# Stick-breaking prompt attention: one sigmoid and value differences in place of two sigmoids and a product

## What is computed

```
z = einsum('bqhd,bshd->bhqs', q, k) * 64 ** -0.5          # valid where s < t
log_keep = where(valid, log_sigmoid(-z), 0)
log_rest = cumsum(log_keep, reverse) - log_keep
a = where(valid, exp(log_sigmoid(z) + log_rest), 0)
o = einsum('bhqs,bshd->bqhd', a, v)
```

## Time and profile before

| | |
|---|---|
| median of three runs | 1863.23 us |
| profiled execution, its own time | 1862.8 us |
| its span, first to last instruction | 1861.1 us |
| granted TensorE clock, mean | 0.969 |
| PE / PEld busy share of the span | 92% / 87% |
| DVE / ACT / POOL busy share | 42% / 26% / 33% |

### The profile page before, as it was taken

How to read it: one execution, slowest core, us unless ns; L and a number is a source line. 1 busy time by engine, 2 the same in 40 slices (tenths; PEclk the granted TensorE clock), 3 DMA queues, 4 the chain that set the end, 5 groups by cost and what they waited for, 6 DMA issues and landing times.

```text
span 1861.1 us, 33169 instructions
## 1 busy us (share of the span) xinstructions
PE 1715.9 (92%) x14512; PEld 1612.1 (87%) x14512; DVE 772.6 (42%) x956; ACT 492.9 (26%) x938; POOL 610.9 (33%) x340
## 2 busy tenths in 40 slices
PE   4999999997988758878999999999999999999998
PEld 3998989995556447767999999999999999999898
DVE  5553033556888457883134222222222121226322
ACT  5232113225766535532132000000000000003211
POOL 4232322322332022324234444444443343442520
PEclk9999999998999968997999999999999999999999
DMA  5112311114000444533321111111111111112221
GB/s 174 49 47 70 101 62 61 66 58 140 1 2 1 149 93 103 114 71 74 91 59 45 46 46 46 46 46 46 46 46 46 46 46 46 46 46 69 57 57 49
DMA packets 202662, 116.50 MB, mean 63 GB/s; under 512 B 74449, under 2 KB 196765, under 8 KB 202525
## 3 DMA queue, kind: packets, MB, share of 16 engines
q1 hardware_dynamic: 193024, 101.45, 19.3%
q10 hardware_dynamic: 9500, 13.02, 1.9%
HBM read 92.60 MB, written 21.84 MB: 61 GB/s over the span
## 4 chain that ended last, share of the span: by engine, by line
PE 77%; DVE 8%; issue 5%; ACT 4%; SPq 3%; DMA 3%; POOL 1%; ACTq 0%; DVEq 0%; POOLq 0%
PE psum L2127 44%; PE psum L1938 8%; PE psum L2419 5%; PE psum L1907 3%; PE psum L1908 3%; PE psum L1909 3%; PE psum L1969 2%; PE psum L1977 2%; PE psum L1990 2%; DVE area L1668 2%; DMA area<-x_scratch 1%; PE psum L2438 1%; DVE area L1509 1%; DVE act_lo L1810 1%; DVE area L1672 1%
## 5 line engine op out<-in xcount | busy, mean ns | idle before, releaser
L2127 PE MATMUL psum<-act_hi,w_round 128*128 128x352 f32 x1920 | 368.5, 325 | 0.7 <-ACT area L1329 0.4
L954 POOL TENSOR_TENSOR w_round<-w_plain,ones 128x1024 fp32r<-128x1024 f32 x80 | 169.8, 2122 | 512.2 <-DMA w_plain<-in_w_up_dram 227.1
L2127 PEld LDWEIGHTS psum<-act_hi,w_round 128*128 128x128 f32 x1920 | 320.6, 189 | 1.8 <-issue 1.0
L2127 PE MATMUL psum<-hid_hi,w_round 128*128 128x352 f32 x1344 | 257.6, 323 | 0.4 <-DVE hid_lo L1840 0.4
L2127 PEld LDWEIGHTS psum<-hid_hi,w_round 128*128 128x128 f32 x1344 | 222.4, 188 | 0.7 <-DVE hid_lo L1840 0.7
L1817 DVE TENSOR_TENSOR area<-psum,area 128x1056 f32<-128x1056 f32 x72 | 90.6, 1258 | 309.5 <-PE psum L2127 309.5
L2127 PE MATMUL psum<-act_lo,w_round 128*128 128x352 f32 x960 | 207.0, 324 | 0.0
L955 POOL TENSOR_TENSOR w_round<-w_plain,w_round 128x1024 fp32r<-128x1024 f32 x80 | 204.3, 2554 | 6.3
L1428 ACT ACTIVATE hid_hi<-area 128x1056 fp32r<-128x1056 f32 x28 | 30.5, 1088 | 589.1 <-DVE area L1833 589.1
L1907 PE MATMUL psum<-w_round,act_hi 128*128 128x256 f32 (+1 forms) x576 | 166.1, 288 | 6.7 <-POOLq L904 3.6
L1908 PE MATMUL psum<-w_round,act_hi 128*128 128x256 f32 (+1 forms) x576 | 163.4, 284 | 0.0
(11 more groups left out here) (298 smaller groups left out, 2666.3 us busy)
## 6 DMA issues: line engine op xcount, KB each, us to landing
w_plain<-in_w_up_dram SPq DMA_DIRECT2D x32, 512.0 KB, 3.9
w_plain<-in_w_down_dram SPq DMA_DIRECT2D x32, 512.0 KB, 3.4
w_plain<-in_w_in_dram SPq DMA_DIRECT2D x14, 1024.0 KB, 5.4
conv_scratch<-area ACTq DMA_DIRECT2D x12, 512.0 KB, 2.7
area<-in_x_prompt_dram SPq DMA_DIRECT2D x8, 512.0 KB, 3.6
w_plain<-in_cache_k_dram SPq DMA_DIRECT2D x4, 1024.0 KB, 5.4
w_plain<-in_w_out_dram SPq DMA_DIRECT2D x8, 512.0 KB, 5.0
w_plain<-in_x_prompt_dram SPq DMA_DIRECT2D x8, 512.0 KB, 4.7
```

What stands on the lines that cost most here:

```text
L954: own.link(pool.tensor_tensor(hi, ring_raw(n), ones[:, 0:1].to_broadcast([P, RB]), ALU.mult))
L2127: last = pe.matmul(bank(bank_set(tile) + c)[:, 0:CH], w(k), a(k)[:, CH * c:CH * (c + 1)], start=(begins and k == ks[0] and w is w_h and a ...
```

## The change

It removes the query stage, the second sigmoid and the product. `keep_buf` after the running product holds R itself, is transposed, and multiplies the differences of neighbouring values, v_(s-1) - v_s (`v_diff`, with zero before the first); one product of v with the identity adds the query's own value. `v_diff` is loaded by SP from the stored `v_out`, shifted by a row, in two transfers (127 rows of the first block, then seven blocks), and POOL subtracts `v_tok` from it in eight instructions of 128x512. The scores of both heads of a pair are computed by one call from the two 64-row halves of `q_t` and `k_t`, the loop over u inside that over 512 columns. Buffers move: `keep_buf` is four deep; two `turned_buf` lie elsewhere; so the first loads of the convolution's values, and two memsets on POOL, move behind the attention, and the scratch clears wait for the differences.

```
-        DEEP = 3
-        sig_buf = carve(act_hi_plain, 0, DEEP, TP)
+        DEEP = 4
+        v_diff = carve(act_hi_plain, 0, NT, W)
...
             sp.wait_ge(dense_ready, NC)
+            sp.wait_ge(v_stored, 32)
+            sp.dma_start(v_diff[1:P, 0, :], v_out[0:P - 1, :]).then_inc(vs_loaded[0], 16)
+            sp.dma_start(v_diff[:, 1:NT, :], v_out[P - 1:TP - 1, :].rearrange("(t p) c -> p t c", p=P))\
+              .then_inc(vs_loaded[1], 16)
             cache_values_in(0)
...
             sp.wait_ge(cs_stored, 1 + 32 * NC)
-            conv_v_in(0)
-            conv_v_in(1)
...
             conv_qk_in(0)
             sums_in(0)
+            conv_v_in(0)
+            conv_v_in(1)
...
-            for y in range(STEPS):
-                pool.wait_ge(scores_ready, 1 + earlier(y, 2))
-                pool.tensor_tensor(q_stage[rows, u, :], q_t[rows, i, P * t:P * (t + 1)], ones[rows, :],
-                                   ALU.mult).then_inc(q_staged, 1)
+            for n in range(NT):
+                pool.wait_ge(vs_loaded[n > 0], 16)
+                pool.tensor_tensor(v_diff[:, n, :], v_diff[:, n, :], v_tok[:, n, :], ALU.subtract).then_inc(d_made, 1)
...
                 act.activation(keep_buf[:, n, 0:w], z, ACT.Sigmoid, scale=-(HD ** -0.5))
-                act.activation(sig_buf[:, n, 0:w], z, ACT.Sigmoid, scale=HD ** -0.5).then_inc(sig_made, 1)
...
             for y in range(STEPS):
+                copy_weights(y)
                 if y + DEEP < STEPS:
                     sigmoids(y + DEEP)
-                if y + 1 < STEPS:
-                    copy_weights(y + 1)
...
-                own.link(dve.tensor_tensor_scan(back, back, starts, 0.0, ALU.mult, ALU.max))
-                dve.tensor_tensor(sig[:, 0:w - 1], sig[:, 0:w - 1], keep[:, 1:w], ALU.mult).then_inc(att_made, 1)
+                dve.tensor_tensor_scan(back, back, starts, 0.0, ALU.mult, ALU.max).then_inc(att_made, 1)
...
+            def scores(t):
+                i, w = t // NT, P * (t % NT + 1)
                 for c in range(0, w, 512):
                     n = min(512, w - c)
+                    for u in range(2):
+                        last = pe.matmul(bank(2 * u + c // 512)[:, 0:n],
+                                         q_t[half(u), i, P * (t % NT):P * (t % NT + 1)],
+                                         k_t[half(u), i, c:c + n], start=True, stop=True)
...
             def values(t):
+                pe.wait_ge(o_split, 1 + max(t - 1, 0))
+                for u in range(2):
+                    pe.matmul(bank(6 + t % 2)[half(u), 0:P], v_tok[:, t % NT, first:first + HD], ident[:],
+                              start=True, stop=False)
                 pe.wait_ge(att_placed, 1 + 2 * t + 2)
+                if i == 0:
+                    pe.wait_ge(d_made, t + 1)
...
+            for t in range(STEPS // 2):
+                turn_weights(2 * t)
+                if t + 2 < STEPS // 2:
+                    scores(t + 2)
+                turn_weights(2 * t + 1)
+                if t:
+                    values(t - 1)
```

More of the change, by code:

```diff
@@ L215, in trunk_step @@
         tails_stored = sem("tails_stored")
-        q_staged = sem("q_staged")
+        vs_loaded = [sem("vs_loaded0"), sem("vs_loaded1")]
+        d_made = sem("d_made")
         scores_ready = sem("scores_ready")
@@ L361, in trunk_step @@
         assert SW == 2 * (TP + TS // 2) and 4 * TS == P
-        DEEP = 3
-        sig_buf = carve(act_hi_plain, 0, DEEP, TP)
+        DEEP = 4
         keep_buf = carve(act_lo_plain, 0, DEEP, TP)
[L367 to L370, removed]
+        v_diff = carve(act_hi_plain, 0, NT, W)
+        turned_buf = [w_plain[:, at:at + TP] for at in (2 * BLK, 2 * BLK + TP, 3 * BLK, 4 * BLK + 528)]
         PARTS = 5
@@ L406, in trunk_step @@
         d_lane_t = carve(dn_w, 5632, LB * LB)[0:LANES, :]
-        g_rows = carve(dn_w, 5632, P)[0:NTT * H, :]
+        g_rows = carve(dn_w, 6016, P)[0:NTT * H, :]
         own_key = carve(dn_w, 3072, TP)
@@ L852, in _ @@
             own = Chain(pool, pool_own)
-            pool.sem_inc(q_staged, 1)
             pool.memset(param_rows, 0.0).then_inc(consts_made, 1)
@@ L918, in _ @@
                 own.leave(2)
-            own.link(pool.memset(q_stage, 0.0))
-            for y in range(STEPS):
-                i, u, t = y // UNITS, y % 2, y % UNITS // 2
-                pool.wait_ge(scores_ready, 1 + earlier(y, 2))
-                pool.wait_ge(q_staged, 1 + y)
-                rows = slice(HD * u, HD * (u + 1))
-                pool.tensor_tensor(q_stage[rows, u, :], q_t[rows, i, P * t:P * (t + 1)], ones[rows, :],
-                                   ALU.mult).then_inc(q_staged, 1)
[L929 to L941, removed]
+            pool.wait_ge(dense_ready, NC)
+            own.mark(pool.memset(own_key[:, 0:TP - P], 0.0))
+            own.mark(pool.memset(v_diff[0:1, 0, :], 0.0))
+            own.link(pool.tensor_copy(own_key[:, TP - P:TP], ident[:]))
+            pool.sem_inc(consts_made, 1)
+            for n in range(NT):
+                pool.wait_ge(vs_loaded[n > 0], 16)
+                pool.tensor_tensor(v_diff[:, n, :], v_diff[:, n, :], v_tok[:, n, :], ALU.subtract).then_inc(d_made, 1)
+            pool.memset(zeros, 0.0).then_inc(consts_made, 1)
+            pool.wait_ge(consts_made, 5)
+            pool.wait_ge(o_ready, 1 + STEPS // 2)
+            own.mark(pool.memset(d_cqk[:, :, TS:HD], 0.0))
+            own.link(pool.memset(d_cv[:, 0, :, TS:HD], 0.0))
             def split_ring(n):
@@ L1146, in sigmoids @@
                 n, w = y % DEEP, P * (y % UNITS // 2 + 1)
-                act.wait_ge(scores_ready, 1 + y + 1)
-                act.wait_ge(att_turned, 1 + earlier(y, DEEP))
+                act.wait_ge(scores_ready, 1 + y // 2 + 1)
+                if y >= DEEP:
+                    act.wait_ge(att_turned, 1 + y - DEEP + 1)
                 z = psum[:, 2 * (y % 2):2 * (y % 2) + 2, :].rearrange("p b c -> p (b c)")[:, 0:w]
-                act.activation(keep_buf[:, n, 0:w], z, ACT.Sigmoid, scale=-(HD ** -0.5))
-                act.activation(sig_buf[:, n, 0:w], z, ACT.Sigmoid, scale=HD ** -0.5).then_inc(sig_made, 1)
+                act.activation(keep_buf[:, n, 0:w], z, ACT.Sigmoid, scale=-(HD ** -0.5)).then_inc(sig_made, 1)
             def round_out(t):
@@ L1182, in _ @@
                 act.wait_ge(k_stored[u], 16 * NTT)
-            copy_weights(0)
             for y in range(STEPS):
+                copy_weights(y)
                 if y + DEEP < STEPS:
                     sigmoids(y + DEEP)
-                if y + 1 < STEPS:
-                    copy_weights(y + 1)
-                if y and y % 2 == 0:
+                if y >= 2 and y % 2:
                     round_out(y // 2 - 1)
@@ L1564, in _ @@
                 n, w = y % DEEP, P * (y % UNITS // 2 + 1)
-                keep, sig = keep_buf[:, n, :], sig_buf[:, n, :]
+                keep = keep_buf[:, n, :]
                 dve.wait_ge(sig_made, 1 + y + 1)
@@ L1962, in _ @@
                     last.then_inc(dense_ready, 1)
[L1963 to L1966, removed]
+            def scores(t):
+                i, w = t // NT, P * (t % NT + 1)
+                if t:
+                    pe.wait_ge(sig_made, 1 + 2 * t)
                 for c in range(0, w, 512):
                     n = min(512, w - c)
-                    last = pe.matmul(bank(2 * u + c // 512)[:, 0:n], q_stage[:, u, :], k_t[:, i, c:c + n],
-                                     start=True, stop=True)
+                    for u in range(2):
+                        last = pe.matmul(bank(2 * u + c // 512)[:, 0:n],
+                                         q_t[half(u), i, P * (t % NT):P * (t % NT + 1)],
+                                         k_t[half(u), i, c:c + n], start=True, stop=True)
                 last.then_inc(scores_ready, 1)
@@ L1977, in turn_weights @@
                     last = pe.transpose(bank(4 + n // 4)[:, P * (n % 4):P * (n % 4 + 1)],
-                                        sig_buf[:, y % DEEP, P * n:P * (n + 1)], ident[:])
+                                        keep_buf[:, y % DEEP, P * n:P * (n + 1)], ident[:])
                 last.then_inc(att_turned, 1)
@@ L1983, in values @@
                 i = t // NT
+                pe.wait_ge(o_split, 1 + max(t - 1, 0))
+                for u in range(2):
+                    first = P * i + HD * u
+                    pe.matmul(bank(6 + t % 2)[half(u), 0:P], v_tok[:, t % NT, first:first + HD], ident[:],
+                              start=True, stop=False)
                 pe.wait_ge(att_placed, 1 + 2 * t + 2)
-                pe.wait_ge(o_split, 1 + max(t - 1, 0))
+                if i == 0:
+                    pe.wait_ge(d_made, t + 1)
                 for n in range(t % NT + 1):
-                    rows = P - 1 if n == t % NT else P
                     for u in range(2):
                         first = P * i + HD * u
```

(21 more changed lines are left out.)

## The result

The change makes the kernel faster: 1845.23 us (median of four runs, 1842.63 to 1845.92) against 1863.31; the ratio is 0.9905, 95% interval 0.9888 to 0.9922, so 18 us or 0.95%. The forecast was 1837, 26 us less, in a range from 1820 to 1856. The profiled execution took 1842.63 us, its span 1840.9, which is 20.2 under the span of before.

What follows compares the result with a forecast made beforehand. PE was taken to set the attention's pace, with DVE close behind, and to be the sole bound afterwards. Three later pairs gain 22.5 us and the first 3.5: 26 off 1862.8 gives 1837, own range 1830 to 1849, stated range 1820 to 1856.

Steps and rivals of the forecast that it cites:

- The halves run side by side: Attention scores: two heads' products in 64-row halves run together, two for the price of one, 9.2 us less per pair.
- The list: PE prices by number n of 128-key blocks: scores .21 + .21n us, transposes .19 + .11n, value products .15 + .22n.
- the charge for the change of shape: PE, per query block: one idle of .17 us charged to the scores for changing into row halves.
- The price of a later pair: Attention's later head pairs: PE 32.4 us plus 1.6 of copy wait, 34.0, 7.5 less than 41.5; three pairs 22.5.
- The check of the list: PE prices summed over a pair of the kernel before, n = 1 to 8: 37.1 us against 37.3 measured.
- rival 1: Attention pairs: better overlap, less PE idle, cheaper shape changes; pair near 30.5 us, 39 us saved, about 1824; chance .13.
- DVE and ACT have room: Later pair: DVE falls to 22.3 us, ACT to some 19; PE alone bounds, the others have 10 us of room.
- The first pair: First head pair with start-up: `values(7)` ends at 483.4 instead of 485.3; gain about 3.5 us, range 0 to 6.
- The small load then lands at about 443.5: First pair: the 0.26 MB value load lands at 443.5 by the 1 MB loads' rate, the large near 448.5.
- a sign against it: First pair: `values(1)` should start near 450 us; a start behind 460 would make the forecast wrong.
- rival 2: Differences come late (load 10 us later, queue shared with keys) or copy waits stay larger: 1848 to 1856; chance .14.
- The sum takes nothing: First pair: POOL's eight subtractions could hold DVE 8.3 us, but DVE has room there, so nothing is charged.

## Why the prediction was right, and where it missed

**The halves run side by side: right.** 9.9 us of scores against 17.6 on one half and 18.9 before. The list had a saving of 9.2, or 10.6 us of scores with the charge for the change of shape. Measured are 9.0 saved against the kernel before; 7.7 of them are shown to come from running side by side.

**The price of a later pair: right, and too high.** 34.0 us forecast, 31.9 measured (33.2, 31.9 and 30.4 between the ends of the value products). PE's sum was 32.4 and is 30.5, the wait 1.6 and is 1.4. The excess is in fixed terms added per query block, as the chain of the second pair shows (start us, us, what):

```profile
505.54 0.70 PE psum L1970 x5
506.24 0.37 PE psum L1980 x4
506.61 0.87 PE psum L1988 x16
507.48 0.81 PE psum L1970 x6
508.29 1.92 PE psum L1961 x8
510.20 0.80 PE psum L1970 x6
```

Scores at n = 8 take 1.92, where the list with its charge has .38 + .21 x 8 = 2.06; a set of transposes at n = 6 takes .81, where it has .85. The value products with the query's own product come out as forecast: .37 + .87 = 1.24 at n = 4, and the list has 1.25. So most of the charge for entering row halves does not show, though PE now changes its shape four times per block: the .17, an idle of the weight load in the earlier trace rows, was not a cost to PE here. Some .24 per block, eight times, is the 1.9 us.

The check of the list against the kernel before, 37.1 to 37.3, could not show this, and its agreement is partly chance. The 37.3 were measured at a mean clock of 0.96, while the rows of the list come from a stretch at 1.00 (504 to 515 us); by the mean clock that pair lost some 1.7 us (an estimate, .04 x 41.5). The later pairs now run at 1.00 throughout: PE idled 1.9 of the 4 us ahead of the earlier trace rows, and now 1.4 us in the whole third pair. The row of before, columns as in the earlier trace rows:

```profile
556.00:560.00 4.00, 2.06 (x15) 1.77 (x14) 3.77 (x3) 3.26 (x6) 1.72 (x2) 0.94 0.00 0
```

A list at full clock had that gain in it without saying so. So the three later pairs gained 28.1 us, where the forecast had 22.5; rival 1 gave the direction, with the shape changes costing less than charged.

**DVE and ACT have room: right.** 22.3 and 20.7 us of 31.9. Both parts are needed: with the scores alone the second and third pair stay at 41.7 and 39.1 us behind DVE and ACT, and with the work taken off DVE and ACT but the scores in turn at 43.5 and 39.0 behind PE. Over the last three pairs the scores alone brought 5.4 us and the removed work alone 4.4, and neither made the kernel faster (0.9995 and 1.0033); together they brought 28.1.

**The first pair: the step that failed.** "The small load then lands at about 443.5" took the rate of the 1 MB transfers, 1.05 MB in 2.9 us, for a transfer of another shape. The 127 rows went at a sixteenth of it and landed at 452.5, and the large load behind them near 457. `values(1)` started at 459.0, not near 450 and just short of the 460 that the prediction named as a sign against it. The first pair lost 7.3 us where 3.5 of gain were forecast. Cutting the load gave 9 us back, put `values(0)` at 444.3, near the forecast's 444.5, and the end of the pair at 483.6, near its 483.4: the rest of that reckoning held. The late load is rival 2's condition, but not for its reason: with no keys ahead the load still took 14.2 us. (By rival 2's own terms its time ends at 1853, not 1856.) Of the forecast's 26 us, then, +5.6 came in the later pairs and -10.8 in the first: 20.8 in the profile, 18 in the medians. The total is nearer to the forecast than its two terms are, because they missed in opposite directions; that is luck.

**"The sum takes nothing" for POOL against DVE: right for this kernel, by its delay.** In the changed kernel the loads come so late that the taps run free (0.75 and 1.32 us), and where the subtractions then meet two running products (4.54 us for two of 128x640, while two of 128x768 take 3.40 after them) DVE is not on the chain. With the loads early and cut, the taps are met, and that costs 5 us.

What stays open: the medians differ by 18.1 us and the profiles by 20.2. The part behind the attention is 1252 to 1257 us long in the profiles, from one kernel to the next. The difference sits mostly in the DeltaNet part, whose products in 64x64 corners span 170 to 175 us from first to last, with no change in it that I could name. So differences of 2 to 5 us between the times of these kernels are read from the attention in the traces and not from the times alone.

## What to carry to other kernels

Where several engines stand close together, sum each of them per turn of the loop before and after: here relieving one alone gained 4 to 5 us and both together 28. A transfer's cost hangs on its shape and not on its bytes alone; look at the share of the transfer engines while it is alone. Here cutting 127 rows into 112 and 15 was enough. Data that comes earlier is not always better: the work that it sets off may collide with what was running there, so say when it is to start.

## What was not expected of the hardware

A transfer of 127 rows of 2 KB took 14.2 us with nothing ahead of it (25 GB/s while it was alone), and 112 and 15 rows of the same took 2.3. It also held SP's queue: the next load took 7.94 us to issue and 22.7 to land, and 0.39 and 12.3 with the rows cut. Subtractions of 128x512 on POOL that met DVE's taps took some 2.2 us each in place of 1.26 and lengthened each tap by 0.9 to 1.0 us. Two f32 products of 64 rows and 128 columns, on different row halves and PSUM banks, cost little more than one (9.9 us for 48 records against 17.6 on one half). Behind a stall of the SiLU the same value products took 3.29 us at a granted clock of 0.5 and 1.75 at 1.00.
